# Nine of eleven down blocks of each feed-forward part: seven products of 2x2 block sums for half of the columns

## The chip, the core and the metric

The kernel runs on one core of a Trainium2 chip. The metric is the device time of one execution in microseconds (us). TensorE multiplies, ScalarE and VectorE work on tiles beside it, and the SyncE queue issues the loads of weights.

## What is computed

Two transformer-like blocks over 256 tokens of width 1024, in fp32. The change touches the down product of the two feed-forward parts of the first block:

```python
def _swiglu(h, w_gu, w_down):
    g, u = jnp.split(h @ w_gu, 2, axis=-1)
    return (jax.nn.silu(g) * u) @ w_down          # (256 x 2816) @ (2816 x 1024)
...
x = x + 0.5 * _rmsnorm(_swiglu(_rmsnorm(x, ffn1_pre_g), ffn1_w_gu, ffn1_w_down), ffn1_post_g)
...                                               # the mixer, the cross attention
x = x + 0.5 * _rmsnorm(_swiglu(_rmsnorm(x, ffn2_pre_g), ffn2_w_gu, ffn2_w_down), ffn2_post_g)
```

## The kernel before

All weights come as one stream of blocks of 128 x 2048 elements, in the order in which they are used. A block lands in `w_raw` (ring of three). ScalarE rounds it into `w_hi` (`round_block`, L1364), VectorE takes the remainder `w_lo = w_raw - w_hi` (`low_block`, L2094), and SyncE may then load the block three further on. ScalarE may round block b once TensorE is through with block b - 3. Each product of fp32 matrices is three matmuls (`product`, L524): high x high, high x low and low x high.

A feed-forward part has 22 hidden tiles of 128 features. An up block gives one tile: 48 matmuls of 256 columns (gate and up half, 8 row tiles, 3 matmuls each). A down block takes a pair of tiles: two tiles k, two token halves t, two column halves h of 512, three matmuls each, so 24 matmuls of 512 columns, which add up in four PSUM banks over all eleven down blocks. The stationary operand is the hidden tile (`ffn_hi`, `ffn_lo`), the moving one the weights. The order on TensorE is up 0, 1, 2, down 0, up 3, then a hardware loop of 8 turns (up, down, up), then up 20, down 9, up 21, down 10. The last product of a down block is split into narrower matmuls by `LAST_DOWN` (L761), mostly into halves of 256 columns.

For hidden tile j VectorE (`hidden_tile`, L2226) multiplies the gate half by the root (`pre`, L2235), ScalarE applies Silu (L1425), VectorE multiplies by the up half (L2238, this frees the bank), ScalarE rounds to `ffn_hi` (L1434), and VectorE takes the remainder `ffn_lo` (L2245), for which TensorE waits. Remainders of weight blocks stand between these in an order written out by hand: `hidden_tile(j, between, behind)` puts some ahead of `ffn_lo` and some after it. Part 1 also prepares the normalised memory on VectorE, part 2 the filters of the second block (`kfil`, `kdif`).

Behind the last down block ScalarE sums the squares of the four banks (L1502), VectorE scales them into `ffn_xn` (L2331), computes the inverse root in ten small linked steps and adds to `x` (`residual`, L2338). After part 1 TensorE goes on with four blocks of keys (`kv0` to `kv3`, with transposes of the normalised `x` between the last two); after part 2 with spectra of the filters (`filter_spectrum`, L1039, 12 fp32 matmuls) and then transposes of `x` (`raw_turn`, L625 is its matmul), which wait for the residual.

A bank is claimed in program order (`claim`, L502): TensorE waits until all earlier contents of the bank were read, and all its later instructions queue behind that wait. Up blocks take banks 0, 1 and 2 in turn, the four down sums banks 3 to 6.

## Time and profile before

| | us |
|---|---|
| runs (three) | 1080.31, 1080.8, 1081.05; median 1080.8 |
| profiled execution | 1081.31 |
| span of its instructions | 1079.4 |
| TensorE busy in the span | 1068.7 (99%) |
| VectorE busy | 789.1 (73%) |
| ScalarE busy | 608.5 (56%) |
| feed-forward part 1, and 2 | 15 to 192, 673 to 855 |

The span runs from the first to the last instruction; the execution's own time is longer by what lies around it. The durations of matmuls overlap, so their pace is read from start to start. The granted TensorE clock was 1.00 of full speed (2.4 GHz) in both feed-forward parts.

### The profile page before, as it was taken

The page shows a single profiled execution, that of the slowest core. Times are in us where ns is not written, and L with a number is a line of the kernel's source. Part 1 is how long each engine was busy: PE and PEld are TensorE (multiplying, and loading weights), DVE is VectorE, ACT ScalarE, POOL GpSimd, SP SyncE. Part 2 cuts the span into 40 slices and gives each one's busy share as a digit, 9 for nine tenths or more (in the row PEclk, how much of TensorE's full clock was granted, in tenths as well). Part 3 has the DMA queues.
Part 4 walks back from the last instruction along what each step waited for, and adds up shares of the span by engine and source line. Part 5 has one row for each costly group of instructions (what it writes and reads, how often), then busy time and mean ns, then how long its engine had stood idle before and what let it go on. Part 6 is the DMA issues. An engine that isn't in the chain of part 4 may idle for free.

```text
span 1079.4 us, 21082 instructions
## 1 busy us (share of the span) xinstructions
PE 1068.7 (99%) x8534; PEld 1009.7 (94%) x8534; DVE 789.1 (73%) x1125; ACT 608.5 (56%) x905; POOL 0.2 (0%) x4
## 2 busy tenths in 40 slices
PE   9999999999999999999999999999999999999999
PEld 7999999999989999999999998999999799999898
DVE  5665556989979777778778555775655887997884
ACT  5544444678586545878445556444444575655471
POOL 0000000000000000000000000000000000000000
PEclk9999999999999999999999999999999999999999
DMA  9866556465543454444546533465556355542251
GB/s 343 292 213 211 176 182 209 151 221 174 179 154 121 152 181 157 157 164 149 208 166 244 196 106 130 147 230 198 188 182 212 119 177 200 191 157 95 102 196 39
DMA packets 29297, 190.71 MB, mean 177 GB/s; under 512 B 3656, under 2 KB 4521, under 8 KB 7466
## 3 DMA queue, kind: packets, MB, share of 16 engines
q1 hardware_dynamic: 26480, 182.53, 48.6%
q10 hardware_dynamic: 2746, 7.16, 1.9%
q8 instruction: 54, 0.88, 0.3%
q14 instruction: 17, 0.14, 0.0%
HBM read 188.62 MB, written 1.05 MB: 176 GB/s over the span
## 4 chain that ended last, share of the span: by engine, by line
PE 87%; DVE 9%; ACT 2%; issue 1%; DMA 1%; SPq 0%; DVEq 0%; ACTq 0%
PE bank L526 15%; PE bank L528 15%; PE bank L527 15%; PE bank L538 10%; PE bank L539 10%; PE bank L540 10%; DVE sb_w_lo L2098 3%; PE bank L625 2%; PE bank L761 1%; DVE sb_ssd_conv L2409 1%; DMA sb_w_raw<-in_w 1%; PE bank L709 1%; PE bank L886 1%; ACT sb_w_hi L1371 1%; PE bank L1048 1%
## 5 line engine op out<-in xcount | busy, mean ns | idle before, releaser
L2098 DVE TENSOR_TENSOR sb_w_lo<-sb_w_raw,sb_w_hi 128x2048 fp32r<-128x2048 f32 x169 | 386.4, 2289 | 118.9 <-ACT sb_w_hi L1371 118.5
L1371 ACT ACTIVATE sb_w_hi<-sb_w_raw 128x2048 fp32r<-128x2048 f32 x169 | 322.9, 1911 | 33.0 <-PE bank L528 29.2
L526 PE MATMUL bank<-sb_hT_hi,sb_w_hi 128*128 128x256 f32 (+1 forms) x816 | 225.7, 277 | 0.0
L528 PE MATMUL bank<-sb_hT_hi,sb_w_lo 128*128 128x256 f32 (+1 forms) x816 | 225.7, 277 | 0.0
L527 PE MATMUL bank<-sb_hT_lo,sb_w_hi 128*128 128x256 f32 (+1 forms) x816 | 225.6, 276 | 0.0
L538 PE MATMUL bank<-sb_hT_hi,sb_w_hi 128*128 128x256 f32 (+2 forms) x744 | 213.1, 286 | 0.2 <-DVE sb_hT_lo L2175 0.2
L539 PE MATMUL bank<-sb_hT_lo,sb_w_hi 128*128 128x256 f32 (+2 forms) x744 | 206.2, 277 | 0.0
L540 PE MATMUL bank<-sb_hT_hi,sb_w_lo 128*128 128x256 f32 x744 | 205.9, 277 | 0.0
L526 PEld LDWEIGHTS bank<-sb_hT_hi,sb_w_hi 128*128 128x128 f32 (+1 forms) x816 | 152.7, 187 | 0.0
L528 PEld LDWEIGHTS bank<-sb_hT_hi,sb_w_lo 128*128 128x128 f32 (+1 forms) x816 | 152.6, 187 | 0.0
L527 PEld LDWEIGHTS bank<-sb_hT_lo,sb_w_hi 128*128 128x128 f32 (+1 forms) x816 | 152.6, 187 | 0.0
L538 PEld LDWEIGHTS bank<-sb_hT_hi,sb_w_hi 128*128 128x128 f32 x744 | 140.0, 188 | 3.9 <-issue 2.4
L539 PEld LDWEIGHTS bank<-sb_hT_lo,sb_w_hi 128*128 128x128 f32 x744 | 140.0, 188 | 1.5 <-issue 1.2
L540 PEld LDWEIGHTS bank<-sb_hT_hi,sb_w_lo 128*128 128x128 f32 x744 | 139.8, 188 | 0.0
L1425 ACT ACTIVATE sb_ffn_gate<-sb_ffn_gate 128x256 f32<-128x256 f32 x44 | 18.4, 418 | 133.7 <-DVE sb_ffn_gate L2235 133.7
L526 PE MATMUL bank<-sb_w_hi,sb_ffn_hi 128*128 128x512 f32 x156 | 60.9, 390 | 0.7 <-DVE sb_ffn_lo L2245 0.7
L528 PE MATMUL bank<-sb_w_hi,sb_ffn_lo 128*128 128x512 f32 x156 | 60.8, 390 | 0.0
L527 PE MATMUL bank<-sb_w_lo,sb_ffn_hi 128*128 128x512 f32 x156 | 60.8, 390 | 0.0
L1434 ACT ACTIVATE sb_ffn_hi<-sb_ffn_act 128x256 fp32r<-128x256 f32 x44 | 18.3, 416 | 47.5 <-PE bank L761 34.5
L527 PE MATMUL bank<-sb_w_lo,sb_hT_hi 128*128 128x256 f32 (+1 forms) x136 | 39.9, 293 | 0.0
L528 PE MATMUL bank<-sb_w_hi,sb_hT_lo 128*128 128x256 f32 (+1 forms) x136 | 39.9, 293 | 0.0
L526 PE MATMUL bank<-sb_w_hi,sb_hT_hi 128*128 128x256 f32 (+1 forms) x136 | 39.9, 293 | 0.0
(516 smaller groups left out, 2077.9 us busy)
## 6 DMA issues: line engine op xcount, KB each, us to landing
sb_w_raw<-in_w SPq DMA_DIRECT2D x169, 1024.0 KB, 4.9
sb_w_raw<-in_w SPq DMA_DIRECT2D x4, 512.0 KB, 7.8
sb_hT<-in_xT SPq DMA_DIRECT2D x2, 512.0 KB, 5.3
sb_x<-in_x SPq DMA_DIRECT2D x2, 512.0 KB, 11.8
sb_mem_xn<-in_mem ACTq DMA_DIRECT2D x1, 1024.0 KB, 7.1
sb_mem_T<-in_memT ACTq DMA_DIRECT2D x1, 1024.0 KB, 10.4
sb_post_g<-in_ffn_post_g ACTq DMA_DIRECT2D x2, 512.0 KB, 5.7
sb_decay<-in_c_decay ACTq DMA_DIRECT2D x1, 768.0 KB, 5.3
```

The costliest lines, as they stand in the source:

```text
L526: pe.matmul(o, a_hi, b_hi, start=first, stop=False)
L527: pe.matmul(o, a_hi, b_lo, start=False, stop=False)
L528: return pe.matmul(o, a_lo, b_hi, start=False, stop=last)
L538: pe.matmul(o[:, 0:width + more[0]], stat_hi, moving(move_hi, width + more[0]), start=k == 0, stop=False)
L539: pe.matmul(o[:, 0:width + more[1]], stat_hi, moving(move_lo, width + more[1]), start=False, stop=False)
L540: return pe.matmul(o[:, 0:width], stat_lo, moving(move_hi, width), start=False, stop=k == kt - 1)
L625: return pe.transpose(o, src, ident)
L709: mm = pe.matmul(o[:, i * SEQ:(i + 1) * SEQ], w[:, k, i * P:(i + 1) * P], hT[:, k, :], start=False, stop=k == KD - 1 and i == 1)
L1371: act.activation(w_hi[b % STAGES][:], w_raw[b % RING][:], ACT.Copy).then_inc(w_hi_in, 1)
L1425: act.activation(f["gate"][:, j % 2, :], f["gate"][:, j % 2, :], ACT.Silu).then_inc(S("ffn_gate"), 1)
L1434: act.activation(f["hi"][:, j % 2, :], f["act"][:, j % 2, :], ACT.Copy).then_inc(S("ffn_hi"), 1)
L2098: tt(w_lo[b % STAGES][:], w_raw[b % RING][:], f32(w_hi[b % STAGES][:]), ALU.subtract).then_inc(w_lo_in, 1)
```

## The change

Down blocks 0 and 10 of each part stay plain. For blocks 1 to 9 ("mixed") the columns 512 to 1023 are multiplied as before. The columns 0 to 511 are two blocks of 256, the tokens two blocks of 128, the features two tiles: a 2x2 by 2x2 block product, done with seven products (Winograd's form) instead of eight. For that VectorE builds three sums of weight quarters per block (`mix_block`; ScalarE rounds them, VectorE takes the remainder, 768 columns) and four sums of the hidden tiles' halves (`first_sum`, `other_sums`, 4 x 128 columns, with rounding and remainder). The seven products add up in four banks over all mixed blocks, two of them (5 and 6) for parts that several results share; these are opened with a product by a zero tile. After block 9 `part_copies` (ScalarE) and `join` (VectorE, four operations of 256 columns) put the results together, and behind block 10 they are added to the sums of the plain blocks. Up blocks have two banks left instead of three, and hidden tile 2 of part 1 goes to bank 5. The transposes for the memory's root move into up block 20. The host puts the columns of these weight blocks in another order. The core of the diff:

```diff
@@ constants and places
+MIXED_PAIRS = PAIRS - 2
+MIXED_OF = {down_at(n, c): MIXED_PAIRS * (n - 1) + c - 1 for n in (1, 2) for c in range(1, PAIRS - 1)}
+PLAIN_AT, MIX_AT = 0, 1024
+                "joined": place(40, f"ffn{n}_joined", [P, TOK, 512]),
+                "parts": place(44, f"ffn{n}_parts", [P, 2, 256]),
+        mix_raw = place(40 + LINE, "mix_raw", [P, 768])
+        mix_hi = place(43 + LINE, "mix_hi", [P, 768], F32R)
+        mix_lo = place(46 + LINE, "mix_lo", [P, 768], F32R)
+        sum_raw = place(49 + LINE, "sum_raw", [P, 4, P])
+        sum_hi = place(51.5, "sum_hi", [P, 4, P], F32R)
+        sum_lo = place(53.5, "sum_lo", [P, 4, P], F32R)
+        zero_r = place(55.5, "zero_r", [P, P], F32R)
@@ TensorE
-                o = claim("mem_rb", 7)
+                o = claim("mem_rb", (FIRST["ffn1"] + 1) % 3)
+            def open_mixed(n, q):
+                claim(f"mixed{n}.{q}", 5 + q, down_at(n, PAIRS - 2))
             def ffn_part(n, norm):
+                last_bank = (FIRST[f"ffn{n}"] + 2) % 3
+                down_banks = (3, 7, 4, last_bank)
+                def up_bank(j):
+                    return 5 if n == 1 and j == 2 else (FIRST[f"ffn{n}"] + j % 2) % 3
...
+                def mixed_block(c, turn=0, parts=(512,), all_three=False):
+                    pe.wait_ge(w_lo_in, b + 1 - SPLIT_FROM + TURN * turn)
...
+                    tile_in(c, 0, turn)
+                    plain_half(banks[7], 0, top)
+                    tile_in(c, 1, turn)
+                    plain_half(banks[7], 1, top)
+                    of_tile(5, 0, 0, top, hi, lo, b11, False)
+                    of_tile(3, 0, 1, top, hi, lo, b21, False)
+                    of_tile(4, 0, 1, low, mix_hi, mix_lo, u4, False)
+                    pe.wait_ge(S("ffn_sum_lo"), MIXED_PAIRS * (n - 1) + c + turn)
+                    of_sum(3, 1, 3, hi, lo, b22, False)
+                    of_sum(5, 1, 0, mix_hi, mix_lo, u1, True)
+                    of_sum(6, 0, 1, hi, lo, u2, False)
+                    of_sum(6, 1, 2, mix_hi, mix_lo, u3, True)
+                    plain_half(banks[last_bank], 0, low)
+                    last_product(banks[last_bank], hi[:, last], lo[:, last], parts, all_three).then_inc(block_done, 1)
+                def plain_block(c, parts=(512,), all_three=False):
...
+                        for i in (0, 2, 1, 3) if last and k else range(4):
+                            if first and k and i == 3:
+                                pe.wait_ge(S("zero_r"), n)
+                                for q in range(n):
+                                    open_mixed(n, q)
+                                    pe.matmul(banks[5 + q][:], zero_r[:], hi[:, 0, 0:512], start=True, stop=False)
+                                mm = last_product(o, hi[:, 1, h], lo[:, 1, h], parts, all_three)
...
-                if n == 1:
-                    mem_root_turn()
-                up_block(FF_TILES - 2)
-                down_block(PAIRS - 2, 0, *LAST_DOWN[n][2])
+                up_block(FF_TILES - 2, between=mem_root_turn if n == 1 else None)
+                mixed_block(PAIRS - 2, 0, *LAST_DOWN[n][2])
...
             stay_warm(zeros[:, 0:P], zeros[:], 1)
+            open_mixed(1, 1)
+            pe.matmul(banks[6][:], zeros[:, 0:P], zeros[:], start=True, stop=False)
@@ ScalarE
+                if b in MIXED_OF:
+                    act.wait_ge(S("ffn_mixed"), MIXED_OF[b] + 1 + turn)
+                    act.activation(w_hi[b % STAGES][:], w_raw[b % RING][:], ACT.Copy)
+                    act.activation(mix_hi[:], mix_raw[:], ACT.Copy).then_inc(w_hi_in, 1)
+                def sums_high(c, turn=0):
+                    act.wait_ge(S("ffn_sum"), MIXED_PAIRS * (n - 1) + c + turn)
+                    act.activation(sum_hi[:], sum_raw[:], ACT.Copy).then_inc(S("ffn_sum_hi"), 1)
+                def part_copies():
+                    o = full(act, f"mixed{n}.0")
+                    act.activation(f["joined"][:, 0, 0:256], o[:, 0:256], ACT.Copy)
+                    copy(f"mixed{n}.0", f["parts"][:, 0, :], o[:, 256:512])
@@ VectorE
+                if b in MIXED_OF:
+                    ins = tt(mix_lo[:], mix_raw[:], f32(mix_hi[:]), ALU.subtract)
+            def mix_block(b, turn=0):
...
+                tt(mix_raw[:, 0:512], quarter(0, 2), quarter(1, 3), ALU.add).then_inc(S("ffn_mixing"), 1)
+                dve.wait_ge(S("ffn_mixing"), 2 * p + 1 + 2 * turn)
+                tt(quarter(1, 2), mix_raw[:, 0:256], quarter(2, 3), ALU.add).then_inc(S("ffn_mixing"), 1)
+                dve.wait_ge(S("ffn_mixing"), 2 * p + 2 + 2 * turn)
+                tt(mix_raw[:, 512:768], quarter(1, 2), quarter(3, 4), ALU.add).then_inc(S("ffn_mixed"), 1)
+                def first_sum(c, turn):
+                    tt(sum_raw[:, 2, :], even[:, 0:P], even[:, P:SEQ], ALU.subtract).then_inc(S("ffn_summing"), 1)
+                def other_sums(c, turn):
...
+                    tt(sum_raw[:, 1, :], sum_raw[:, 2, :], odd[:, P:SEQ], ALU.add)
+                    tt(sum_raw[:, 0, :], even[:, P:SEQ], odd[:, P:SEQ], ALU.subtract).then_inc(S("ffn_summing"), 1)
...
+                    tt(sum_raw[:, 3, :], odd[:, 0:P], sum_raw[:, 1, :], ALU.subtract).then_inc(S("ffn_sum"), 1)
+                def sums_low(c, turn):
+                    dve.wait_ge(S("ffn_sum_hi"), p + 1 + turn)
+                    tt(sum_lo[:], sum_raw[:], f32(sum_hi[:]), ALU.subtract).then_inc(S("ffn_sum_lo"), 1)
+                def join():
...
+                    link(tt(w, o[:, 0:256], y[:, 0, 0:256], ALU.subtract))
+                    link(tt(y[:, 0, 256:512], w, p5, ALU.add))
+                    tt(y[:, 1, 0:256], o[:, 256:512], w, ALU.subtract)
+                    read(tt(y[:, 1, 256:512], y[:, 0, 256:512], o[:, 256:512], ALU.subtract), f"mixed{n}.1")
@@ hidden_tile
+                    if mixed:
+                        wait_read(dve, f"up{n}.{j}", turn)
+                        if j % 2:
+                            other_sums(j // 2, turn)
+                    for b in behind:
+                        if b in MIXED_OF:
+                            mix_block(b, turn)
...
+                    if mixed:
+                        (sums_low if j % 2 else first_sum)(j // 2, turn)
...
+                    tt(zero_r[:], zeros[:, 0:P], zeros[:, 0:P], ALU.subtract).then_inc(S("zero_r"), 1)
...
+                    join()
                     hidden_tile(FF_TILES - 1, [], [b + 2], 0, [mem_lows])
...
                     hidden_tile(FF_TILES - 1, [], [])
+                    join()
@@ VectorE, behind the last down block
-                for i in (1, 0, 3, 2):
...
+                for i in (0, 2):
+                    read(tt(y[:, i // 2, :], o[:], y[:, i // 2, :], ALU.add), key)
+                for i in (1, 3):
+                    read(gained(i, full(dve, key)[:]), key)
+                    wait_read(dve, f"down{n}.{i - 1}")
+                    scaled = gained(i - 1, y[:, (i - 1) // 2, :])
```

## Rows read from the trace of the kernel before

**Rows 1.** The page, part 1: busy time, share of the span, instructions of each engine.
```profile
PE 1068.7 (99%) x8534; PEld 1009.7 (94%) x8534; DVE 789.1 (73%) x1125; ACT 608.5 (56%) x905; POOL 0.2 (0%) x4
```
**Rows 2.** Busy time by windows: stretch, its length, engines (instructions), clock, DMA share, GB/s.
```profile
44.20:175.80 131.60, 131.60 (x989) 124.94 (x988) 79.10 (x86) 57.91 (x59) 0.00 (x0) 1.00 0.58 199
175.80:209.40 33.60, 33.56 (x244) 31.44 (x243) 29.55 (x54) 19.15 (x24) 0.00 (x0) 1.00 0.46 157
```
**Rows 3.** Timeline of TensorE (start, duration, instruction): up block, down block, return to 512 columns.
```profile
120.92 0.28 PE L538 MATMUL bank<-sb_hT_hi,sb_w_hi 128*128 128x256 f32 x1
...
126.25 0.28 PE L528 MATMUL bank<-sb_hT_hi,sb_w_lo 128*128 128x256 f32 x1
...
127.51 0.39 PE L528 MATMUL bank<-sb_w_hi,sb_ffn_lo 128*128 128x512 f32 x1
...
130.23 0.39 PE L528 MATMUL bank<-sb_w_hi,sb_ffn_lo 128*128 128x512 f32 x1
...
60.81 0.40 PE L526 MATMUL bank<-sb_w_hi,sb_ffn_hi 128*128 128x512 f32 x1
...
61.51 0.39 PE L526 MATMUL bank<-sb_w_hi,sb_ffn_hi 128*128 128x512 f32 x1
```
**Rows 4.** TensorE, 256 columns behind 512: at `cq`, and the halves of a down block.
```profile
910.29 0.28 PE L526 MATMUL bank<-sb_w_hi,sb_cq_hi 128*128 128x256 f32 x1
...
912.41 0.40 PE L526 MATMUL bank<-sb_w_hi,sb_ckv_hi 128*128 128x512 f32 x1
...
65.82 0.40 PE L761 MATMUL bank<-sb_w_lo,sb_ffn_hi 128*128 128x256 f32 x2
...
66.30 0.29 PE L538 MATMUL bank<-sb_hT_hi,sb_w_hi 128*128 128x256 f32 x1
```
**Rows 5.** TensorE, end of down block 0 of part 1 and start of up block 3.
```profile
32.27 0.39 PE L761 MATMUL bank<-sb_w_hi,sb_ffn_hi 128*128 128x512 f32 x1
...
33.16 0.39 PE L538 MATMUL bank<-sb_hT_hi,sb_w_hi 128*128 128x256 f32 x1
```
**Rows 6.** Timeline of VectorE, hidden tile 2 of part 1 (in brackets idle time, and its end).
```profile
33.02 0.42 DVE L2235 TENSOR_TENSOR sb_ffn_gate<-bank,sb_ffn_rb 128x256 f32<-128x256 f32 x1
33.92 0.42 DVE L2238 TENSOR_TENSOR sb_ffn_act<-bank,sb_ffn_gate 128x256 f32<-128x256 f32 x1 [0.48 <-ACT sb_ffn_gate L1425]
```
**Rows 7.** VectorE at the end of a loop turn and the start of the next.
```profile
75.74 2.29 DVE L2098 TENSOR_TENSOR sb_w_lo<-sb_w_raw,sb_w_hi 128x2048 fp32r<-128x2048 f32 x1 [1.38 <-ACT sb_w_hi L1371]
77.95 0.42 DVE L2235 TENSOR_TENSOR sb_ffn_gate<-bank,sb_ffn_rb 128x256 f32<-128x256 f32 x1
```
**Rows 8.** End of part 1: VectorE's tile 21, TensorE's taking it, TensorE at `kv2`.
```profile
186.94 0.42 DVE L2235 TENSOR_TENSOR sb_ffn_gate<-bank,sb_ffn_rb 128x256 f32<-128x256 f32 x1 [0.96 <-PE bank L528]
188.82 0.42 DVE L2245 TENSOR_TENSOR sb_ffn_lo<-sb_ffn_act,sb_ffn_hi 128x256 fp32r<-128x256 f32 x1 [0.54 <-ACT sb_ffn_hi L1434]
...
189.48 0.40 PE L526 MATMUL bank<-sb_w_hi,sb_ffn_hi 128*128 128x512 f32 x1
...
203.44 0.28 PE L528 MATMUL bank<-sb_mem_hi,sb_w_lo 128*128 128x256 f32 x1
203.76 0.38 PE L538 MATMUL bank<-sb_mem_hi,sb_w_hi 128*128 128x256 f32 x1
```
**Rows 9.** End of part 2: VectorE to the last scaling, TensorE's transposes.
```profile
849.61 0.42 DVE L2235 TENSOR_TENSOR sb_ffn_gate<-bank,sb_ffn_rb 128x256 f32<-128x256 f32 x1 [0.18 <-PE bank L528]
...
851.49 0.43 DVE L2245 TENSOR_TENSOR sb_ffn_lo<-sb_ffn_act,sb_ffn_hi 128x256 fp32r<-128x256 f32 x1 [0.54 <-ACT sb_ffn_hi L1434]
851.83 1.22 DVE L2210 TENSOR_TENSOR sb_kfil<-sb_kfil 128x1024 f32<-128x1024 f32 x1
853.82 2.00 DVE L2331 SCALAR_TENSOR_TENSOR sb_ffn_xn<-bank,sb_post_g 128x512 f32<-128x512 f32 x3 [0.77 <-PE bank L528]
856.16 0.69 DVE L2331 SCALAR_TENSOR_TENSOR sb_ffn_xn<-bank,sb_post_g 128x512 f32<-128x512 f32 x1 [0.34 <-ACT sb_ffn_junk L1502]
...
860.39 0.63 PE L625 MATMUL bank<-sb_square,sb_x 128*128 128x128 f32 x4
```

More of the change, by code:

```diff
@@ L746, in down_block @@
+                def plain_block(c, parts=(512,), all_three=False):
+                    b = down_at(n, c)
+                    first, last = c == 0, c == PAIRS - 1
+                    pe.wait_ge(w_lo_in, b + 1 - SPLIT_FROM)
                     hi, lo = halves(b, 2, D)
+                    if first:
+                        for i in range(4):
+                            claim(f"down{n}.{i}", down_banks[i], down_at(n, PAIRS - 1) if i == 3 else None)
                     for k in range(2):
-                        pe.wait_ge(S("ffn_lo"), FF_TILES * (n - 1) + 2 * c + 1 + k + 2 * turn)
@@ L764, in down_block @@
+                            if last and k == 1 and i < 3:
                                 ends(mm, f"down{n}.{i}")
@@ L768, in ffn_part @@
                     up_block(j, between=(lambda: root_turn(n)) if j == 3 - n else None)
-                o = [claim(f"down{n}.{i}", 3 + i, down_at(n, PAIRS - 1) if i == 3 else None) for i in range(4)]
-                down_block(0, 0, *LAST_DOWN[n][0])
+                plain_block(0, *LAST_DOWN[n][0])
                 up_block(3)
@@ L1454, in ffn_part @@
                 high(3)
+                sums_high(1)
                 after(up_at(n, 3))
@@ L1469, in ffn_part @@
                     high(5, turn)
+                    sums_high(2, turn)
                     round_block(b + 2, turn)
@@ L3103 @@
             at += m
+    for n in MIXED_OF:
+        top, low = stream[n, :, 0:1024].copy(), stream[n, :, 1024:2048].copy()
+        stream[n] = np.concatenate([top[:, 512:], low[:, 512:], top[:, 0:512], low[:, 256:512], low[:, 0:256]], axis=1)
     arrays["w"] = stream
```

112 lines of the change are left out of this document (79 added, 33 removed).

## The prediction

> **What bounds the kernel now.** I read the page first: TensorE is busy for 99% of the span and VectorE for 73% [rows 1]. So less work for TensorE is time won, provided nobody makes it wait. Then the table by windows, since an average over stages hides where VectorE is full: in the loop of the first feed-forward part TensorE is busy for all of 131.60 us and VectorE for 79.10 (60%), but in the 33.6 us behind it VectorE is busy for 29.55 (88%) [rows 2]. Then the timeline, for three things: the rhythm of matmuls (start to start, since their durations overlap), the places where TensorE takes something from VectorE just in time, and how late VectorE is there. The reader is to see that the gain lies in the loops and that VectorE's new work is long at three places that have no cover.
>
> **What a mixed block saves.** Inside a down block twelve matmuls of 512 columns take 2.72 us, 0.2267 each; in an up block 47 matmuls of 256 columns take 5.33 us, 0.1134 each [rows 3]. Both cost the same per column. A down block has 24 matmuls of 512 columns. The mixed block keeps 12 of them and replaces the other 12 by 7 products x 3 = 21 matmuls of 256. At 0.1134 that would be 12 x 0.2267 - 21 x 0.1134 = 2.72 - 2.38 = 0.34 us less. But 256-column matmuls that follow 512-column ones have another rhythm: behind `cq` 18 of them take 2.12 us, 0.118 each, and the four halves at the end of a down block, whose stationary operand is `ffn_hi`, take 0.48 us, 0.120 each [rows 4]. The nine products of tiles (3 x 3) have that stationary operand, so I take 0.120; the twelve of sums resemble `cq`, so 0.118: 1.08 + 1.42 = 2.50 us. On going back to 512 columns the first three take 0.70 us instead of 0.68 [rows 3]. A block then gains 2.72 - 2.50 - 0.02 = 0.20 us; the bounds are 0.18 (all at 0.120) and 0.34. Over 18 blocks: 3.7 us gained, from 3.3 to 6.1.
>
> The Trainium skill has another price ("TensorE: Matmul & The Clock Gate", Back-to-back issue gap): N columns take N/2.4 ns plus 2.5, so 215.8 and 109.2 ns. By it a block would gain 12 x 0.2158 - 21 x 0.1092 = 0.30 us, an estimate, and the 18 blocks 5.3 us; the whole sum would end at about 1085. The rows above differ from it for both widths, and no run here shows its figures.
>
> After a mixed block comes the same sequence as now (three 512s, then six halves), and behind it the up block runs at 0.1134 [rows 3]. I take no change for the up blocks; if they stayed at 0.118, see the third rival.
>
> **Openers.** One 512-column matmul by `zero_r` in part 1 and two in part 2, 0.227 each: 0.68 us lost. The fp32 one on bank 6 at the very start runs while TensorE waits for the input; I cost it nothing, at most 0.9.
>
> **Part 1, the beginning.** The tile `zero_r` (128 columns, below the 0.42 us of a 256-column operation [rows 6]) stands on VectorE before hidden tile 0, whose result TensorE already waits for: 0.2 us lost. More important: hidden tile 2 now lies in bank 5, and mixed sum 0 is opened in bank 5 inside the first plain block, ahead of its last product. That claim waits until VectorE has read bank 5, and everything of TensorE is queued behind it. VectorE reaches hidden tile 2 at 33.02 without idle time, because the weight remainder of block 4 precedes it, and its second operation, which frees the bank, ends at 33.92 + 0.42 = 34.34 [rows 6]. TensorE is at the last product at 32.27 [rows 5]. Both move by 0.2 with `zero_r`. The stall is 2.1 us; about 0.2 of it was there as a wait for block 4 just behind (TensorE's next block starts at 33.16, and 32.27 plus three matmuls is 32.95 [rows 5]). Net 1.9 us lost. Nothing hides it.
>
> **The loop.** VectorE gets three weight sums per turn (512, 256, 256 columns, with links 0.69 + 0.46 + 0.38, 1.5 us), the remainder of 768 columns (between 0.69 for 512 and 1.22 for 1024 [rows 9], so 0.95), four stationary sums of 128 (0.2 to 0.3 each, 0.9 in all) and a remainder of 512 (0.65): 4 us on top of 9.9 per 16.4 us turn. It fits. ScalarE gets copies of 768 and 512, some 1.4 us at VectorE's price; it is busy for 57.91 of 131.60 us [rows 2] and has room. What moves is the end of the turn. The weight sums fill idle time that the weight remainder spends waiting for ScalarE (1.38 us [rows 7]) and cost nothing there. The copy and remainder of 768 delay hidden tile 5 by 0.8 + 0.95, less 0.9 of idle time ahead of it: 0.85. Then ScalarE's last weight copy of the turn waits 0.2 for the stationary sums and 0.5 for copying them: together the last weight remainder ends about 1.5 us later than now. Now hidden tile 4 starts at 77.95, some 0.5 after it could [rows 7]; after the change some 2.0. The next up block needs its weights 2 us or more after that, so in a full turn TensorE does not wait. At the start of part 2, and of the loop in part 1, where VectorE has filter and memory work too, the weight sums push a weight remainder past its need: I take 0.3 + 0.3 in part 2 and 0.1 in part 1, from walking the order of the two queues with these durations, and 0.1 for `up2` in part 2, which waits for the bank of `up0` as only two banks are left: 0.8 us lost, between 0 and 2.
>
> **The end of part 1.** Here VectorE has no room. The remainder of hidden tile 21 starts at 188.82 and is ready at 189.24, and TensorE takes it at 189.48 [rows 8]: 0.2 us of slack. Before hidden tile 21 VectorE is idle for 0.96 us [rows 8]. The change brings the lateness of the loop (1.5) and `join`, four operations of 256 columns, the first two linked: 0.46 + 0.46 + 0.33 + 0.33 = 1.6 us. 1.5 + 1.6 - 0.96 - 0.2 = 1.9 us of stall in the middle of the last plain block. Behind it VectorE has six operations of 512 columns (two additions, four scalings) instead of four: 2 x 0.65 = 1.3 (three take 2.00 with the next overlapping [rows 9]), less some 0.5 of idle time between the four now, 0.8 us. The residual follows, then the weight remainder for `kv2`, for which TensorE already waits: 0.32 us between two starts where 0.118 is the rhythm [rows 8]. So the 0.8 is lost again.
>
> **The end of part 2.** The remainder of hidden tile 21 starts at 851.49 and is ready at 851.92. Idle time before hidden tile 21 is 0.18 [rows 9], and the slack is taken to be 0.1, a little less than in part 1. `join` stands behind this tile here. So 1.5 - 0.18 - 0.1 = 1.2 us stall. Then from the tile's end to the end of the last scaling VectorE now takes 856.85 - 851.92 = 4.9 us with some 1.1 idle [rows 9]; afterwards 1.6 (`join`) + 1.2 (`fold_sum`) + 6 x 0.65 = 6.7, without idle, so 1.8 more. TensorE's transposes at 860.39 [rows 9] come behind that chain. A part of the 1.8 (0.25) is my rounding up of overlapping starts, and I take 1.55 us lost. ScalarE's squares precede its copies of the spectra, so `spec4` waits too, but inside this same wait.
>
> **The sum.** Gained: 3.7. Lost: openers 0.7, `zero_r` 0.2, bank 5 1.9, weight order 0.8, ends of part 1 1.9 + 0.8, ends of part 2 1.2 + 1.55. Lost in all 9.05; net 5.35 us slower. The profiled execution took 1081.31 us around a span of 1079.4, 0.5 above the median of the runs shown (1080.8). Its own sum gives 1086.7; for the median I predict 1086.2. If all new products ran at 0.1134, 2.4 us more would be gained, but TensorE would meet the waits for VectorE earlier and give about a third back: 1084.6. With the losses a quarter smaller or larger (6.8 to 11.3) and the gain between its bounds, the forecast's own range is 1083 to 1089.5.
>
> **Rivals.**
> (1) Faster, one mechanism: VectorE's new work is absorbed. The waits named (bank 5; hidden tile 21 twice; the residual twice) total 7.35 us; they vanish if VectorE comes through its queue some 2 us earlier at each of these places than the rows say. Then 9.05 - 7.35 = 1.7 lost and 3.7 to 6.1 gained: 1076.4 to 1078.8. The change turns faster once fewer than 2 us of waits remain. For it: 52 us of idle VectorE time per loop [rows 2]. Against: that time lies before the waits, not in them, and the order within the queue is fixed.
> (2) The products of sums and tiles run at 0.1134 because their operands' addresses suit (the diff gives the stationary sums another offset within 512 bytes than `ffn_hi` has): 1084.6, still slower. Included above.
> (3) The up blocks after a mixed block stay at 0.118: 96 x 0.0045 = 0.43 us per turn, 18 turns, less about 1.7 of waits that a slower TensorE absorbs: 6.1 more, 1092.3. For it: the rhythm of a later block here depends on what precedes it [rows 4]. Against: behind the same closing halves the rows show 0.1134 [rows 3].
> (4) The change doesn't do what it says: the block is no shorter, which is so when a 256-column matmul takes 2.72 / 21 = 0.13 us. The count of 12 + 21 follows from the code, and no row shows more than 0.120. Time: 1080.8 + 9.05 = 1089.9.
>
> **Chances.** Forecast with rival 2: 0.70. Rival 1: 0.13, plus 0.05 for a mixture that ends within 2 us of before. Rival 3: 0.09. Rival 4: 0.03. Less than 0.2% (2.2 us) can hardly be told from no change. Faster by more than that 0.13; within it 0.08 (the mixture, and 0.03 of the forecast's lower end); slower 0.79. The range: 1080.5 to 1091.0; below it lies rival 1, above it most of rival 3.
>
> **What would show it.** Right: a wait of TensorE for VectorE of 2 us near 34 in front of the `zero_r` matmul; one of 1 to 2 us for `ffn_lo` near 191 and near 853; transposes of part 2 some 7 us after the last down matmul instead of 5.5; turns of 16.2 instead of 16.4 us, with the 21 matmuls at 0.118 to 0.120. Wrong: no wait at bank 5, a turn that isn't shorter, or up blocks at 0.118 all through the loop.

## The result, and the profile after

| | before | after |
|---|---|---|
| median of the runs (us) | 1080.72 (4 runs) | 1088.71 (4 runs: 1087.72, 1088.13, 1089.29, 1090.82) |
| ratio, 95% interval | | 1.0077, 1.0059 to 1.0094 |
| profiled execution, span | 1081.31, 1079.4 | 1089.29, 1086.5 |

The change makes the kernel 8.0 us slower; 5.4 were forecast, so 1086.2 for the median. In the span of the profiled executions it is 7.1. The page of the kernel after, part 1, to be read beside [rows 1] (busy time, share, instructions):

```profile
PE 1067.7 (98%) x8701; PEld 1014.7 (93%) x8701; DVE 862.3 (79%) x1301; ACT 634.8 (58%) x945; POOL 0.2 (0%) x4
```

TensorE has 1 us less of busy time, VectorE 73 us more. The span grew because TensorE waits, and the view of its waits names for whom (engine, tile and line waited for: us in all, times, longest). Of the kernel after:

```profile
PE bank L540 <- DVE sb_ffn_lo L2409: 4.7, 3, 2.3
PE bank L840 <- DVE sb_ffn_act L2394: 2.0, 1, 2.0
...
PE bank L552 <- DVE sb_w_lo L2200: 1.3, 3, 0.9
PE bank L639 <- DVE sb_x L2530: 1.0, 1, 1.0
PE bank L1130 <- ACT sb_half L1483: 0.8, 1, 0.8
```

The same view of the kernel before has, for these tiles, one wait of 0.7:

```profile
PE bank L709 <- DMA sb_w_raw<-in_w: 0.9, 1, 0.9
...
PE bank L526 <- DVE sb_ffn_lo L2245: 0.7, 1, 0.7
```

The waits stand where the prediction put them. TensorE's timeline of the kernel after (start, duration, in brackets idle time and what ended it) at bank 5, at hidden tile 21 of part 1, at `kv2`, at tile 21 of part 2 and at the transposes behind it:

```profile
31.11 0.39 PE L542 MATMUL bank<-sb_w_hi,sb_ffn_lo 128*128 128x512 f32 x1
33.52 0.77 PE L840 MATMUL bank<-sb_w_hi,sb_zero_r 128*128 128x512 f32 x1 [2.03 <-DVE sb_ffn_act L2394]
34.09 0.63 PE L775 MATMUL bank<-sb_w_hi,sb_ffn_hi 128*128 128x512 f32 x1
...
189.73 0.39 PE L542 MATMUL bank<-sb_w_hi,sb_ffn_lo 128*128 128x512 f32 x1
...
192.37 0.50 PE L540 MATMUL bank<-sb_w_hi,sb_ffn_hi 128*128 128x512 f32 x1 [2.26 <-DVE sb_ffn_lo L2409]
...
207.61 0.39 PE L552 MATMUL bank<-sb_mem_hi,sb_w_hi 128*128 128x256 f32 x1 [0.90 <-DVE sb_w_lo L2200]
...
856.88 0.50 PE L540 MATMUL bank<-sb_w_hi,sb_ffn_hi 128*128 128x512 f32 x1 [1.24 <-DVE sb_ffn_lo L2409]
...
867.10 0.41 PE L639 MATMUL bank<-sb_square,sb_x 128*128 128x128 f32 x2 [1.01 <-DVE sb_x L2530]
```

One thing stood in no step of the prediction: from 33.52 on, the matmuls start 0.43 us apart at 512 columns. Windows of the kernel after (columns as in [rows 2]; the second and third answer to its two rows):

```profile
33.50:36.90 3.40, 3.38 (x13) 3.11 (x14) 3.33 (x4) 2.51 (x3) 0.00 (x0) 0.50 1.01 349
44.20:175.80 131.60, 131.47 (x1079) 128.19 (x1078) 108.33 (x159) 70.03 (x76) 0.00 (x0) 1.00 0.58 199
175.80:209.40 33.60, 30.45 (x225) 28.44 (x224) 30.20 (x51) 21.07 (x28) 0.00 (x0) 1.00 0.41 137
```

The granted clock is 0.50 for 3.4 us, 1.2 instead of 2.4 GHz. TensorE is busy all through, so its matmuls there take 1.7 us longer than at full clock (what that costs the kernel is less, see the first experiment). Directly before it TensorE had stood idle for 2.03 us (the wait for bank 5), and for 1.17 us seven us earlier.

And the gain: TensorE's timeline inside a mixed block. First matmuls of four products, from which the rhythm is read:

```profile
128.99 0.28 PE L540 MATMUL bank<-sb_w_hi,sb_ffn_hi 128*128 128x256 f32 x1
...
129.71 0.28 PE L540 MATMUL bank<-sb_mix_hi,sb_ffn_hi 128*128 128x256 f32 x1
...
130.07 0.28 PE L540 MATMUL bank<-sb_w_hi,sb_sum_hi 128*128 128x256 f32 x1
...
131.43 0.40 PE L540 MATMUL bank<-sb_w_hi,sb_ffn_hi 128*128 128x512 f32 x1
```

The nine matmuls whose stationary operand is the tile take 1.08 us, 0.120 each; the twelve of the sums 131.43 - 130.07 = 1.36, 0.1133 each, not 0.118.

VectorE is busy for 108.33 of the 131.60 us of the loop's window (82%), but it has no time left in a turn. The starts of two hidden tiles one turn apart, in the kernel after:

```profile
115.58 0.42 DVE L2391 TENSOR_TENSOR sb_ffn_gate<-bank,sb_ffn_rb 128x256 f32<-128x256 f32 x1
...
131.43 0.42 DVE L2391 TENSOR_TENSOR sb_ffn_gate<-bank,sb_ffn_rb 128x256 f32<-128x256 f32 x1
```

VectorE's turn takes 15.85 us, TensorE's 16.11. In the loops of the kernel after no idle time of VectorE was ended by TensorE, only by ScalarE, which in turn waited mostly for VectorE's results; before, VectorE waited 0.91 us for TensorE in every turn (its waits from 66 to 164 us: in all, times, longest):

```profile
DVE sb_ffn_gate L2235 <- PE bank L528: 5.5, 6, 0.9
```

So a delay of VectorE ahead of the loop shrinks by only 0.27 us a turn.

Where the 7.04 us between the last matmuls' starts (1076.46 and 1083.50) arise, by stages between starts of TensorE's blocks in the timelines (us; the first row is a time, the others lengths):

| stage | before | after | difference |
|---|---|---|---|
| up to the second half of up block 2, part 1 | 23.77 | 22.30 | -1.5 |
| to the end of down block 2 (2 mixed) | 42.53 | 46.08 | +3.5 |
| down blocks 3 to 8 with their up blocks | 98.32 | 96.68 | -1.6 |
| to the keys (1 mixed) | 27.63 | 30.19 | +2.6 |
| `kv0` to the transposes | 17.08 | 17.94 | +0.9 |
| mixer and attention, to part 2 | 464.27 | 464.27 | 0.0 |
| part 2, from its start to the end of down block 1 (1 mixed) | 39.22 | 40.76 | +1.5 |
| down blocks 2 to 9 with their up blocks | 131.06 | 128.99 | -2.1 |
| to the last down matmul | 10.83 | 12.30 | +1.5 |
| to the transposes | 5.68 | 7.60 | +1.9 |
| the rest | 216.08 | 216.40 | +0.3 |

The first row is no effect of the change that I can show: TensorE waited 0.9 us for the first load of weights in the one execution and not in the other (the row of waits above), and the experiments' executions lie between 21.96 and 24.09 there. Some 0.5 of it is given back in the second row, where TensorE, being earlier, waits 1.17 instead of 0.66 us for a hidden tile.

### The profile page after: what moved, and what is told of

Its sections match the earlier page's. It is cut to its first block, busy times and chain, and to the rows that moved or that the text cites. A ratio compares the mean times of both kernels' runs of the same rounds, so it can differ in the third digit from the quotient of the medians.

```text
span 1086.5 us, 21767 instructions
## 1 busy us (share of the span) xinstructions
PE 1067.7 (98%) x8701; PEld 1014.7 (93%) x8701; DVE 862.3 (79%) x1301; ACT 634.8 (58%) x945; POOL 0.2 (0%) x4
## 4 chain that ended last, share of the span: by engine, by line
PE 71%; DVE 16%; issue 6%; ACT 6%; DMA 1%; DVEq 0%; ACTq 0%
PE bank L542 12%; PE bank L541 12%; PE bank L540 12%; PE bank L552 9%; PE bank L553 8%; PE bank L554 8%; DVE sb_w_lo L2200 5%; ACT sb_w_hi L1459 3%; PE bank L639 2%; DVE sb_ssd_conv L2594 1%; DVE sb_ffn_act L2394 1%; PE bank L968 1%; ACT sb_ffn_gate L1513 1%; PE bank L775 1%; DVE sb_ffn_gate L2391 1%
## 5 line engine op out<-in xcount | busy, mean ns | idle before, releaser
L1459 ACT ACTIVATE sb_w_hi<-sb_w_raw 128x2048 fp32r<-128x2048 f32 x151 | 288.6, 1911 | 31.6 <-PE bank L542 29.0
L540 PE MATMUL bank<-sb_w_hi,sb_ffn_hi 128*128 128x512 f32 (+1 forms) x120 | 43.3, 361 | 4.7 <-DVE sb_ffn_lo L2409 4.7
L541 PE MATMUL bank<-sb_w_lo,sb_ffn_hi 128*128 128x512 f32 (+1 forms) x120 | 43.2, 360 | 0.0
L542 PE MATMUL bank<-sb_w_hi,sb_ffn_lo 128*128 128x512 f32 (+1 forms) x120 | 43.0, 358 | 0.0
L2594 DVE SCALAR_TENSOR_TENSOR sb_ssd_conv<-bank,sb_cols,sb_ssd_conv 128x255 f32<-128x255 f32 (+2 forms) x72 | 34.7, 481 | 6.7 <-ACT sb_ssd_conv L1700 4.5
```

Of the source, the lines that this page charges most:

```text
L540: pe.matmul(o, a_hi, b_hi, start=first, stop=False)
L541: pe.matmul(o, a_hi, b_lo, start=False, stop=False)
L542: return pe.matmul(o, a_lo, b_hi, start=False, stop=last)
L1459: act.activation(w_hi[b % STAGES][:], w_raw[b % RING][:], ACT.Copy).then_inc(w_hi_in, 1)
L2594: ins = stt(v[:, j:SEQ], u[:, 0:SEQ - j], col("ssd_conv_w", taps * ch + taps - 1 - j), v[:, j:SEQ], ALU.mult, ALU.add)
```

## Experiments

Each run has its own executions of the kernel before beside it, on the same chip, with medians from 1079.93 to 1081.09; times are to be read against those (given as "before").

**Is the wait for bank 5 on the path, and does the clock fall because of it?** In the first kernel mixed sum 0 is opened later; in the second TensorE is kept busy in the wait.

```diff
-                                for q in range(n):
+                                for q in range(2 * n - 2):
                                     open_mixed(n, q)
...
-                up_block(3)
+                up_block(3, between=open_late if n == 1 else None)   # claims bank 5, matmul by zero_r
```

> The changed kernel, but in part 1 mixed sum 0 is opened in the middle of up block 3 instead of inside down block 0, so that TensorE reaches the claim of bank 5 after VectorE has read hidden tile 2 out of it. Theory (the wait for the bank is on the path, and the stretch of 3.41 us at half clock right behind it is its consequence): no gap near 31 to 33.5, mean granted clock 1.000, the 2.4 us gap and 1.6 us of slow matmuls both gone, less what other waits just behind take back: 3 to 4 us less than the changed kernel, about 1085.2 (ratio to the kernel before 1.0040). Rival A (the low clock has another cause, such as the load of the input or the wait of 1.4 us at 25): the clock record stays and only the gap goes, 1.5 to 2.4 us less, about 1086.8. Rival B (the wait hides behind the next one, for the weights and the hidden tile): less than 0.5 us gained.

Measured: 1089.13 (before 1079.93), ratio 1.0080 (1.0066 to 1.0094), against 1.0077. Nothing is gained. Its waits of TensorE, and its windows:

```profile
PE bank L540 <- DVE sb_ffn_lo L2414: 6.1, 3, 2.7
PE bank L552 <- DVE sb_w_lo L2205: 2.6, 3, 2.2
...
58.50 0.38 PE L552 MATMUL bank<-sb_hT_hi,sb_w_hi 128*128 128x256 f32 x1 [2.18 <-DVE sb_w_lo L2205]
...
33.50:36.90 3.40, 3.36 (x28) 3.15 (x27) 2.81 (x7) 2.54 (x4) 0.00 (x0) 1.00 1.04 425
194.40:197.90 3.50, 3.50 (x11) 2.75 (x10) 3.50 (x3) 0.17 (x1) 0.00 (x0) 0.51 0.00 0
```

The wait at 31 is gone and comes back at 56, 2.18 us long, for a weight remainder: in front of the loop VectorE computes the memory's root (3.4 us) and has by then no idle time left. (The 2.7 us are the wait for a hidden tile at 28.20, ahead of the edit; this execution came there 1.7 us later than that of the kernel after.) And the stretch of half clock is gone from 33 and stands at 194, behind the wait for tile 21.

How much the wait and the clock cost is best read from TensorE's start of down block 0 to its end of down block 2. Two later kernels, those of `e6_tail_out` and `e7_end1_order`, do there exactly what the changed kernel does, and their traces have the wait for bank 5 (2.04 and 2.02 us) at full clock. They take 41.05 and 41.06 us; this kernel, without the wait, takes 41.08; the changed kernel with the half clock 41.92. In the trace of `e6_tail_out`, from 25 to 68 us:

```profile
PE bank L840 <- DVE sb_ffn_act L2391: 2.0, 1, 2.0
...
PE bank L552 <- DVE sb_w_lo L2200: 0.5, 1, 0.5
```

So rival B is right on the wait: it only hid the next one, and its price is nothing. The half clock cost 0.9 us and not 1.7: the wait of 0.5 us that stands at 56 otherwise is not there behind the slower matmuls. That the clock falls because of this wait is not shown: of five traces with the wait for bank 5 two have the half clock behind it (the changed kernel and `e3_sums_line`), three don't.

```diff
+                                for q in range(10 if n == 1 else 0):
+                                    pe.matmul(banks[6][:], zero_r[:], hi[:, 0, 0:512], start=False, stop=False)
```

> The changed kernel with ten matmuls of 512 columns by the zero tile into bank 6 (they add zero) ahead of the claim of bank 5, 2.27 us: the wait keeps its length, but TensorE is busy in it. Theory (the clock falls because TensorE stands idle for 2.4 us there): the clock stays at 1.000 and the following matmuls run at 0.227 and 0.113 us, so 1.6 us less than the profile of the changed kernel, 1087.1 for the median where the execution had the low clock. Rival A (cause elsewhere): the record of half clock stays, time unchanged at 1088.7. Rival B (matmuls cost more than they fill, since part of the wait is already covered): time up by at most 0.3 us, clock as in A or the theory.

Measured: 1088.38 (before 1079.93), ratio 1.0088 (1.0074 to 1.0101). The clock is full at 33 in its trace, as the theory had it, but half near 193 instead, so its mean is no better (1.000 in two of five runs, 0.997 or 0.998 in three). The median is close to rival A's. Three of five traces with the unfilled wait are at full clock at 33 as well, so this one trace can't tell whether the filling did anything; it did not pay.

**What sets the rhythm of 256 columns?**

```diff
-        sum_hi = place(51.5, "sum_hi", [P, 4, P], F32R)
-        sum_lo = place(53.5, "sum_lo", [P, 4, P], F32R)
+        sum_hi = place(51 + LINE, "sum_hi", [P, 4, P], F32R)
+        sum_lo = place(53 + LINE, "sum_lo", [P, 4, P], F32R)
```

> The changed kernel with the stationary sums (high and low) moved back 448 bytes, to the offset within 512 bytes that the hidden tile's high and low parts have (64). Theory (the rhythm of a 256-column matmul behind 512-column ones hangs on the stationary operand's offset: 0.120 for the tiles at 64, 0.1133 for the sums at 0): the twelve products of sums go from 0.1133 to 0.118 to 0.120 us, 12 x 0.0055 x 18 = 1.2 us slower, about 1089.8. Rival (the rhythm hangs on how long ago the 512-column matmuls were, or on reading from one bank after another): the twelve stay at 0.1133 and the time at 1088.7.

Measured: 1088.30 (before 1079.93), too near to tell; the trace decides. The twelve matmuls of sums start at 131.20, the next one of 512 columns at 132.64:

```profile
131.20 0.28 PE L540 MATMUL bank<-sb_w_hi,sb_sum_hi 128*128 128x256 f32 x1
...
132.64 0.40 PE L540 MATMUL bank<-sb_w_hi,sb_ffn_hi 128*128 128x512 f32 x1
```

1.44 us, 0.120 each: the sums' offset decides over their own rhythm. Six turns take 97.16 instead of 96.68.

```diff
-                "hi": place(24 + LINE, f"ffn{n}_hi", [P, 2, SEQ], F32R),
-                "lo": place(26 + LINE, f"ffn{n}_lo", [P, 2, SEQ], F32R),
+                "hi": place(24, f"ffn{n}_hi", [P, 2, SEQ], F32R),
+                "lo": place(26, f"ffn{n}_lo", [P, 2, SEQ], F32R),
```

> The changed kernel with the hidden tile's high and low parts moved 64 bytes down, to offset 0 within 512 bytes. Theory (offset decides): the nine 256-column products of tiles go from 0.119 to 0.1133 and the six halves at the block's end from 0.118 to 0.1133: 15 x 0.0055 x 18 = 1.5 us faster in the loops, some of it taken back by waits for VectorE, about 1087.5. The 512-column matmuls inside the mixed block, now at 0.229 to 0.232 instead of 0.2267, may gain too: 12 x 0.003 x 18 = 0.6 us. Rival (the width change decides): no rhythm changes, 1088.7.

Measured: 1093.77 (before 1079.93), 5 us slower than the changed kernel. Both theories missed. In the mixed block the 21 matmuls now take 0.118, and the up blocks behind it don't return to 0.1134 [rows 3]: from the first of these rows to the second 47 matmuls start in 5.53 us, 0.1177 each:

```profile
120.73 0.28 PE L540 MATMUL bank<-sb_hT_hi,sb_w_hi 128*128 128x256 f32 x1
...
126.26 0.28 PE L542 MATMUL bank<-sb_hT_hi,sb_w_lo 128*128 128x256 f32 x1
```

A turn takes 99.40 / 6 = 16.57 instead of 16.11 us. That is what the third rival of the prediction described, at about its price of 0.43 a turn, brought about by an address and not by the mixed blocks. Offset 0 is thus not the faster one as such: here tiles and sums both have it. How the offset does it stays open.

**Is TensorE's gain there when nobody makes it wait?** TensorE's program stays (mixed sum 0 is opened late, as in the first experiment), all sums, `join` and the additions are left out (and with them those parts of the result).

```diff
-                    pe.wait_ge(S("ffn_sum_lo"), MIXED_PAIRS * (n - 1) + c + turn)
...
-                        product(..., sum_hi[:, i, :], sum_lo[:, i, :], m_hi[:, m], m_lo[:, m], ...)
+                        product(..., f["hi"][:, s, t], f["lo"][:, s, t], hi[:, m], lo[:, m], ...)
```

> TensorE's program as in the changed kernel (the same 12 matmuls of 512 and 21 of 256 columns per mixed block, the openers, the late opener of the first experiment), but VectorE and ScalarE do none of the new work: no weight sums, no stationary sums, no join, no additions; the seven products read the hidden tiles and the plain weights instead. The sums, and with them the results of the feed-forward parts, are left out. Theory (TensorE gains what its rhythm says, and the whole loss is waits for VectorE): the stationary operands are all at offset 64, so a block gains 2.72 - 21 x 0.119 - 0.02 = 0.20 us; 18 x 0.20 - 0.7 (openers) - 0.2 (zero tile) = 2.7 us faster than before, and 1.2 more if the rhythm of the sums stays at 0.1133: 1077.2, or 1076. Rival (TensorE's own program costs the time, by banks, widths or openers): slower than before, over 1082.

Measured: 1078.66 (before 1080.57), ratio 0.9991 (0.9982 to 1.0000), ten runs of two kinds: six at clock 1.000 (1077.90 to 1078.79) and four at 0.998 (1080.17 to 1081.53), 2.5 us apart. The six are 2.1 us faster than before, where 2.7 were expected: the gain is there. A turn is 0.19 us shorter with all stationary operands at offset 64, as the 0.20 forecast for 0.119 to 0.120. Part 2's start is 0.7 slower than before even here: 0.46 are the openers, 0.45 come with the claim of bank 0 (the 72 matmuls around it start 0.1212 instead of 0.1149 us apart on average: 0.16 us of it is the gap at the claim, the rest the rhythm of 0.118 to 0.120 of the 48 behind it), less one block's 0.2.

**What do `join` and the additions cost?**

```diff
-                    link(tt(w, o[:, 0:256], y[:, 0, 0:256], ALU.subtract))
-                    link(tt(y[:, 0, 256:512], w, p5, ALU.add))
-                    tt(y[:, 1, 0:256], o[:, 256:512], w, ALU.subtract)
-                    read(tt(y[:, 1, 256:512], ...), f"mixed{n}.1")
+                    read(tt(w[:, 0:8], o[:, 0:8], p5[:, 0:8], ALU.subtract), f"mixed{n}.1")
...
-                    read(tt(y[:, i // 2, :], o[:], y[:, i // 2, :], ALU.add), key)
```

> The changed kernel without join (one operation of 8 columns stands for its four), without ScalarE's copy of 256 columns for it, and without the two additions of 512 columns behind each part; the part sums are left out of the result. What stays is the loop with all its sums. Theory (the ends cost 1.9 + 0.8 in part 1 and 1.2 + 1.55 in part 2, of which join and the additions carry 1.6 + 0.8 and 0 + 1.55, and 1.2 of ffn_lo in part 2 belong to the loop's lateness): 4 us less than the changed kernel, about 1084.7. Rival (another piece of VectorE's work takes their place, as the late opener showed): under 1.5 us less, above 1087.

Measured: 1084.24 (before 1080.57), ratio 1.0039 (1.0024 to 1.0055): 4.5 us less than the changed kernel where 4 were expected. By stages of the two traces in which the clock was full, it is 4.1: 1.5 at the end of part 1, 1.0 behind it, 0 and 1.7 at the end of part 2. TensorE's waits, against 4.7 and 1.0 above:

```profile
PE bank L540 <- DVE sb_ffn_lo L2406: 2.7, 3, 1.3
...
PE bank L639 <- DVE sb_x L2519: 0.4, 1, 0.4
```

**Does it help to move that work?**

```diff
-                    join()
                     hidden_tile(FF_TILES - 1, [], [b + 2], 0, [mem_lows])
+                    join()
...
+                if i_post == 0:
+                    low_after(down_at(1, PAIRS - 1))      # kv2's weights, ahead of the residual
```

> The changed kernel with two steps of VectorE moved at the end of part 1: join behind hidden tile 21 and the weights of kv1 instead of ahead of that tile, and the weights of kv2 ahead of the residual's last three operations instead of behind them. Theory (TensorE waits for both in turn): the wait for tile 21 falls from 2.3 to 0.7 us and the one in front of kv2 (1.2) stays below 0.5, since its weights come 2.6 us earlier: 2.3 us less, 1086.4. Rival (VectorE is full from 192 to 209, so a piece moved only moves the wait): the wait for tile 21 falls but the 1.6 us return in front of kv2 or at the transposes behind it; 1088.2 or more.

Measured: 1088.51 (before 1080.57). The rival: the wait for tile 21 falls by 1.7 us and the one at `kv2` goes, and the transposes behind `kv2` get a new one:

```profile
PE bank L639 <- DVE sb_mix_xn L2275: 1.3, 1, 1.3
```

VectorE is full from tile 21 on. Taking work away gained 4.5 us, moving it within the full stretch nothing.

**Fewer mixed blocks, and VectorE's work in the last turn.**

```diff
-MIXED_PAIRS = PAIRS - 2
+MIXED_PAIRS = PAIRS - 3
...
-                with dve.Fori(0, PAIR_TURNS) as turn:
+                with dve.Fori(0, PAIR_TURNS - 1) as turn:
...
+                    hidden_tile(18, [b], [b + 1], 0, [lambda: None, mem_root])
+                    hidden_tile(19, [], [b + 2])
...
+                join()
```

> Eight mixed blocks per part instead of nine: block 9 is plain, so that VectorE and ScalarE make no sums behind the loop. The last turn of the loop is written out, and VectorE takes into it what stood at the full places: the root of the memory's norm (3.4 us, before the loop until now), join, and four of the filters' products; the last filter sum stands ahead of hidden tile 21; bank 5 is opened in up block 3, the zero tile is made in idle time, and kv2's weights stand ahead of the residual. Theory (what makes the changed kernel slow is only where VectorE's work stands): TensorE's gain of 16 x 0.27 = 4.3 less 0.7 for the openers stays, and the waits at 25 to 36, 190, 206 and 855 shrink below what the kernel before had; behind part 2 remain 1.3 us of additions against 1.2 us of the filter sum moved away: 1077 to 1078. Rival (the waits come back at other places because VectorE's total in the parts is too large): 1082 or more.

Measured: 1083.91 (before 1080.57), ratio 1.0031 (1.0019 to 1.0043); at full clock 1081.59 and 1082.60. 4.8 us better than the changed kernel, but the rival's figure. In the trace the 72 matmuls behind the late opener run at 0.118, the memory's root now comes 1.0 us late for its transposes at 170, and TensorE idles 1.0 for tile 21.

```diff
-                                    pe.matmul(banks[5 + q][:], zero_r[:], hi[:, 0, 0:512], start=True, stop=False)
...
+                                m_hi[:, m], m_lo[:, m], c == 1 and side == 0 and bank > 4, closes and c == PAIRS - 3)
```

> The eight-block kernel without openers: TensorE's first and last mixed blocks are written out, the first starts banks 5 and 6 itself, so the zero tile and its three matmuls (0.68 us) go, hidden tile 2 lies in bank 5 in both parts (0.45 us of waiting for bank 0 in up 2 of part 2 go), and VectorE's root of the memory's norm, join and all filter sums but the first two products stand in the last written-out turn, where VectorE waits for ScalarE or has no sums to make. Theory (the rest of the loss is openers, the rhythm of 0.118 behind them, and VectorE's work at full places): from the eight-block kernel's 1081.6 at full clock, 0.7 openers, 0.5 rhythm, 0.45 bank, 1.0 of weight waits at the start of part 2, 1.3 for the memory's root and 1.2 at hidden tile 21 less: 1076.5 at full clock, about 2.4 more where a stretch of half clock falls into the run. Rival (another place of VectorE becomes late instead): 1080 or more.

Measured: 1082.15 (before 1080.73), ratio 1.0015 (1.0006 to 1.0024). Again the rival's figure. The start of part 2 now takes 38.94 (before 39.22; the changed kernel 40.76), but I had put the last filter sum ahead of tile 21. TensorE's timeline there, and the window behind it:

```profile
848.51 0.39 PE L542 MATMUL bank<-sb_w_hi,sb_ffn_lo 128*128 128x512 f32 x1
851.35 0.79 PE L540 MATMUL bank<-sb_w_hi,sb_ffn_hi 128*128 128x512 f32 x1 [2.45 <-DVE sb_ffn_lo L2420]
...
851.20:854.60 3.40, 3.25 (x8) 2.62 (x9) 1.07 (x3) 2.16 (x3) 0.00 (x0) 0.53 0.30 128
```

An idle stretch of 2.45 us, and half clock from 851.0 on, 0.4 us before it ends. With the sum behind tile 21 and the memory's transposes behind up block 20:

> The kernel without openers with two steps put back: in part 2 the second half of the filters' difference and their last sum stand behind hidden tile 21 instead of ahead of it, where VectorE now waits 1.8 us for TensorE, and in part 1 the transposes of the memory's root stand behind up block 20 instead of inside it. Theory (each of TensorE's two remaining waits, 2.8 us at 848.5 with a stretch of half clock behind it and 0.9 us at 170, is VectorE's order alone): both waits go, the half clock with the first, 2.6 + 1.6 + 0.8 = 5 us less than the profiled 1082.4, less 0.5 for the usual start of that product: about 1077.8, faster than the kernel before by 2.5 to 3 us. Rival (the waits move to the next place, the ones behind tile 21 and the residual): 1080 or more.

Measured: 1079.94 (before 1080.58), ratio 0.9995 (0.9986 to 1.0005), the clock full in every run. No difference from the kernel before that can be told, so the forecast of 1077.8 failed and the rival's 1080 is nearly met; 8.8 us better than the change as it was made. One of the eleven runs took 4057.37 us, for no reason that the record shows; it is not in the ratio. What still waits:

```profile
PE bank L540 <- DVE sb_ffn_lo L2422: 1.9, 3, 0.7
...
PE bank L639 <- DVE sb_x L2546: 0.9, 1, 0.9
```

> The kernel above with three steps of VectorE moved from ahead of hidden tile 21 to behind it or into idle time: in part 1 three of the eight scalings of the memory (1.27 us) stand behind tile 21 and two (0.88) inside tile 20's wait for ScalarE; in part 2 one product of the filters (0.7) stands in tile 20's wait and the first half of the difference (0.7) behind tile 21. Theory (the waits of 0.75 and 0.9 us that are left for tile 21 in the two parts are these pieces): both fall below 0.2 us, 1.4 us less than the kernel above, 1078.5, ratio 0.998. Rival (what stands behind tile 21 then delays the keys and the residual by as much): unchanged, 1079.9.

Measured: 1080.58 (before 1081.09), ratio 1.0000 (0.9991 to 1.0009). The waits for tile 21 are gone, as the theory had it, and the time is unchanged, as the rival had it: the transposes behind `kv2` wait again.

```profile
208.55 0.33 PE L639 MATMUL bank<-sb_square,sb_mix_xn 128*128 128x128 f32 x1 [1.31 <-DVE sb_mix_xn L2289]
```

**Is it the order or the products?** The kernel before, with VectorE's order of the kernel without openers:

> The kernel before, with plain down blocks throughout, and only VectorE's order of the kernel above: last turn of its loop written out, the memory's root, the filters' sums and differences in it, kv2's weights ahead of the residual. It tells how much of the gain of the kernel above is order and how much is the seven products. Theory: before has waits of 0.7 us for the filter sums near 708, some 1.0 at the end of part 2 (tile 21, filter sum) and 0.2 at kv2, so order alone gives 1 to 1.5 us: 1079.3. Rival: nothing, since these waits hide one another: 1080.7.

Measured: 1080.42 (before 1080.73), ratio 0.9998 (0.9989 to 1.0007): order alone gives nothing. (It is the order of the kernel without openers; that of the last two versions was not run with plain blocks.)

## Why the prediction came out as it did

The sign, the places of the waits and most of their lengths were right. The forecast for the profiled execution was 1086.7; it took 1089.3. The forecast's own range was added up wrongly: losses of 6.8 to 11.3 and gains of 3.3 to 6.1 give 1081.5 to 1088.8, not 1083 to 1089.5, and the median of 1088.71 lies just inside. Step by step, with the step's stage in the table:

- **The gain** was mis-sized: 0.20 us a block forecast, 98.32 - 96.68 = 1.64 over six turns, 0.27, and 2.07 over eight, 0.26, measured. 18 blocks give some 4.8, not 3.7. The term that failed is "the twelve of sums resemble `cq`, so 0.118": they take 0.1133. Rival 2's reason, the addresses, is right for the sums; moved back 448 bytes they take 0.120. The up blocks don't suffer (rival 3: two of them take 10.90 us before and after), the block is shorter (rival 4: 5.21 instead of 5.49).
- **Bank 5**: forecast a stall of 2.1, measured 33.52 - 31.11 - 0.23 = 2.2. "Nothing hides it" and the 1.9 lost were wrong in their consequence: it delays TensorE ahead of another wait for VectorE at 56, so taking it away gained nothing. A wait's length is not its price when a later wait for the same engine stands behind it. That the term still fits the sum is luck in part: the stretch is longer by what VectorE's queue takes up to the loop, with or without bank 5 (from the start of down block 0 to the end of down block 2 38.88 before, 41.05 at full clock after).
- **The clock** is in no step: it lengthened matmuls by 1.7 us in the profiled execution and the stage by 0.9. [Rows 2] showed it at 1.00 in both windows, and I took that for granted with waits of 2 us added. It was 1.000 in all runs of the kernel before, and below in three of four after.
- **Openers and zero tile**: a matmul of 0.23 us each, as forecast (in part 2 two, 0.46; that of part 1 fell into the half clock). Making the zero tile held VectorE up by 0.21 us directly ahead of hidden tile 0, as forecast (0.2).
- **Weight order**: forecast 0.8, too little. In part 2 alone the stage grew by 1.5, with one mixed block's gain in it 1.8: openers 0.46, the claim of bank 0 about 0.45 where I had put 0.1, and two waits for weight remainders, 0.5 and 0.4 where I had put 0.3 each.
- **The loop's lateness**: forecast that VectorE ends a turn 1.5 us later than before. Hidden tile 20 starts 3.25 us after its up block's end instead of 1.29 in part 1 and 3.07 instead of 1.46 in part 2, so 2.0 and 1.6. The prediction took a fixed delay; in fact VectorE enters the loop of part 1 late and catches up 0.27 us a turn. This is why the stall for tile 21 came out longer in part 1.
- **End of part 1**: forecast 1.9 of stall for tile 21; TensorE idles 2.26 (the product starts 2.4 late), and the stage grew by 2.6 with a block's gain in it. Behind it 0.8 forecast, 0.9 measured.
- **End of part 2**: forecast 1.2, idle time measured 1.24 and the stage 1.5 longer; then 1.55 forecast, 7.60 - 5.68 = 1.9 measured, in two waits: 0.8 for ScalarE at the spectra, 1.0 for `x` at the transposes.

Rival 1 (VectorE absorbs its new work) fails: the waits stand at the instructions that the queue's order named, and their idle times are within 0.4 us of the forecast lengths. That the parts' ends carry 4 us was confirmed by taking the work away (4.5 in the medians, 4.1 in the stages).

Why a repaired version (`e11_late_sum`) only reaches the kernel before: against it, by the stages of the two traces, eight mixed blocks win 1.6 and 1.9 us in the two loops and 0.9 and 0.3 in front of them, and give back 1.0 and 0.9 in front of tile 21's part of the last blocks and 0.8 at the last transposes. Another 1.1 us stand between the transposes behind `kv2` and part 2 (462.41 against 461.34, and 461.1 to 462.4 over the experiments). Half of it is again a wait for VectorE: directly behind the transposes `kv3` starts after 2.17 instead of 1.66 us, having waited for a weight remainder, and so it does (2.10 to 2.20) in each of the five versions with mixed blocks that have `kv2`'s weights ahead of the residual. The cause of the other half, in the mixer and attention, which no edit touched, stays open. The two executions are 1.6 us apart, the medians 0.6. The forecasts of 1076.5, 1077.8 and 1078.5 failed because I treated waits at full places as removable one by one.

## What to carry to other kernels

When a cheaper product for TensorE needs sums by VectorE, what counts is not VectorE's share (82% in the loop) but the length of its queue's turn (15.85 of 16.11 us) and the stretches where it is full and TensorE takes its results just in time, here mostly the ends of stages: work taken out of them counted in full, work moved within them came back at the next wait. A wait for a busy engine may only be hiding the next wait for the same engine; price it by taking it out, or by walking both queues on past it. And TensorE's clock can fall near an added wait: here some runs had 3.4 us of half clock, and that too has to be priced by its stage and not by its own length.

## What the hardware showed that was not expected

- In five traces the granted clock fell to 0.50 for one stretch of 3.4 us inside the kernel, each time between 0.4 us before and 1.4 us behind the end of an idle time of TensorE of 2.0 to 2.5 us: at 33.5 in the kernel after and at 34.4 in `e3_sums_line`, both behind the wait for bank 5; at 194.5 and 192.7 in `e1_open_late` and `e2_fill`, behind the wait for tile 21; at 851.0 in `e9_no_openers`, before a wait of 2.45 ended. It doesn't follow each such wait: that of 2.26 at 192 in the kernel after, those of 2.68 and 2.18 at 28 and 58 in `e1_open_late`, and those for bank 5 in three other traces had full clock. And it differs from run to run of one program. Programs whose traced execution has shorter waits show a mean granted clock below 1 in some runs too: four of ten in `e5_no_sums` (1.6 in the feed-forward parts at most), four of six in `e8_eight_mixed` (1.0), one of eleven in `e12_tile21`; none of them was caught in a trace. With no wait in the feed-forward parts longer than 0.9 us the clock stayed full in 11 runs of 11 (`e11_late_sum`). The Trainium skill ("TensorE: Matmul & The Clock Gate", Part 1) says that an idle array's clock goes down to half, and of its rise to full speed that the moment differs between runs. The traces agree with the first, and the fall differs between runs here as well.
- The rhythm of 256-column matmuls depends on where their stationary operand starts: sums at offset 0 within 512 bytes 0.1133, at 64 0.120, while hidden tiles moved to 0 made everything behind them 0.118, up blocks and sums included. Why is not shown.
- The openers were unnecessary: the first mixed block can start its banks, and the bank's other half needs no start of its own. That is as the Trainium skill has it ("Advanced Engine Details and Errata", PSUM Accumulation: starting clears the marks of the whole bank, and unmarked elements are overwritten). It saves three matmuls of 0.23 us; in part 2 down block 0 takes 5.48 us in `e9_no_openers` instead of 5.96.
